# Two-pass sums of the stick and of the query/key squares, three mask matmuls in place of four, and the final norm's product on POOL, in a two-block decoder kernel

## The reference

```python
q = rms_norm(q.reshape(bsz, seq, ATTN_HEADS, HEAD_DIM), q_norm_g[layer])
k = rms_norm(k.reshape(bsz, seq, ATTN_HEADS, HEAD_DIM), k_norm_g[layer])
...
z = jnp.einsum("bqhd,bkhd->bhqk", qb, kb) * scale
mask = s_idx < t_idx
log_beta = jax.nn.log_sigmoid(z)
log_one_minus = jnp.where(mask, jax.nn.log_sigmoid(-z), 0.0)
tail = lax.cumsum(log_one_minus, axis=3, reverse=True) - log_one_minus
weights = jnp.where(mask, jnp.exp(log_beta + tail), 0.0)
outs.append(jnp.einsum("bhqk,bkhd->bqhd", weights, vb))
```

## Time and profile before

| | us |
|---|---|
| median of three runs | 1236.39 |
| the profiled execution | 1236.73 |
| its span, first to last instruction | 1235.0 |
| outside the span | 1.73 |
| PE busy | 1223.8 (99%) |
| DVE, ACT, POOL busy | 601.2, 505.1, 574.2 |

### The profile page before, as it was taken

How to read it: one execution, slowest core, us unless ns; L and a number is a source line. 1 busy time by engine, 2 the same in 40 slices (tenths; PEclk the granted TensorE clock), 3 DMA queues, 4 the chain that set the end, 5 groups by cost and what they waited for, 6 DMA issues and landing times.

```text
span 1235.0 us, 16489 instructions
## 1 busy us (share of the span) xinstructions
PE 1223.8 (99%) x5598; PEld 1004.6 (81%) x5598; DVE 601.2 (49%) x877; ACT 505.1 (41%) x674; POOL 574.2 (46%) x465
## 2 busy tenths in 40 slices
PE   9999999999999999999999999999999999999998
PEld 7888888888888888888888886768888888888887
DVE  6782435434653166414575879785334213321431
ACT  7532543343443144313473237666333223332331
POOL 5775553233445344453465441134454444444444
PEclk9999999999999999999999999999999999999999
DMA  8343332112333322232133321102232323223222
GB/s 298 124 145 126 118 103 69 51 69 68 102 102 104 102 85 93 94 119 84 64 124 104 101 86 51 35 18 85 71 104 98 117 88 102 86 85 120 81 76 81
DMA packets 34034, 118.41 MB, mean 96 GB/s; under 512 B 4032, under 2 KB 4160, under 8 KB 33856
## 3 DMA queue, kind: packets, MB, share of 16 engines
q1 hardware_dynamic: 33696, 117.49, 28.6%
q10 hardware_dynamic: 288, 0.24, 0.1%
HBM read 115.61 MB, written 2.10 MB: 95 GB/s over the span
## 4 chain that ended last, share of the span: by engine, by line
PE 95%; ACT 2%; DVE 1%; POOL 1%; issue 1%; DMA 0%; SPq 0%; POOLq 0%; ACTq 0%; DVEq 0%
PE ps L1240 29%; PE ps L1241 29%; PE ps L1242 29%; PE ps L1562 1%; PE ps L1407 1%; PE ps L1545 1%; PE ps L1298 1%; PE ps L1297 1%; PE ps L1296 1%; PE ps L1518 0%; PE ps L1306 0%; POOL w_lo L363 0%; PE ps L1603 0%; ACT slab L654 0%; POOL squares L431 0%
## 5 line engine op out<-in xcount | busy, mean ns | idle before, releaser
L363 POOL TENSOR_TENSOR w_lo<-w_raw,w_hi 128x512 fp32r<-128x512 f32 x430 | 555.3, 1315 | 621.8 <-ACT w_hi L464 355.7
L1240 PE MATMUL ps<-xg_hi,w_hi 128*128 128x512 f32 x960 | 375.7, 391 | 0.0
L1242 PE MATMUL ps<-xg_hi,w_lo 128*128 128x512 f32 x960 | 373.7, 389 | 0.0
L1241 PE MATMUL ps<-xg_lo,w_hi 128*128 128x512 f32 x960 | 373.6, 389 | 0.0
L1240 PE MATMUL ps<-y_hi,w_hi 128*128 128x512 f32 (+1 forms) x608 | 230.8, 380 | 0.0
L1241 PE MATMUL ps<-y_lo,w_hi 128*128 128x512 f32 (+1 forms) x608 | 229.8, 378 | 0.0
L1242 PE MATMUL ps<-y_hi,w_lo 128*128 128x512 f32 (+1 forms) x608 | 229.8, 378 | 0.0
L1240 PEld LDWEIGHTS ps<-xg_hi,w_hi 128*128 128x128 f32 x960 | 180.3, 188 | 37.8 <-issue 0.8
L1242 PEld LDWEIGHTS ps<-xg_hi,w_lo 128*128 128x128 f32 x960 | 180.2, 188 | 37.5
L1241 PEld LDWEIGHTS ps<-xg_lo,w_hi 128*128 128x128 f32 x960 | 180.3, 188 | 37.3 <-issue 0.5
L464 ACT ACTIVATE w_hi<-w_raw 128x1024 fp32r<-128x1024 f32 x124 | 130.5, 1053 | 126.0 <-PE ps L1242 126.0
(11 more groups left out here) (210 smaller groups left out, 1058.1 us busy)
## 6 DMA issues: line engine op xcount, KB each, us to landing
w_raw<-weights SPq DMA_DIRECT2D x199, 512.0 KB, 3.3
w_raw<-weights SPq DMA_DIRECT2D x16, 384.0 KB, 2.9
out_t<-h SPq DMA_DIRECT2D x8, 256.0 KB, 2.1
h<-x_t SPq DMA_DIRECT2D x3, 512.0 KB, 8.4
slab<-mem_t SPq DMA_DIRECT2D x2, 512.0 KB, 10.1
slab<-mats_in SPq DMA_DIRECT2D x1, 1024.0 KB, 7.3
w_raw<-weights SPq DMA_DIRECT2D x2, 256.0 KB, 3.9
h<-x_t SPq DMA_DIRECT2D x2, 256.0 KB, 4.4
```

Source lines behind the costliest of these rows:

```text
L363: nc.gpsimd.tensor_tensor(w_lo[:, s, half], w_raw[:, s, half], w_hi[:, s, half].bitcast(F32), ALU.subtract).then_inc(done, 1)
L1240: pe.matmul(out, w[0], x[0], start=first, stop=False)
L1241: pe.matmul(out, w[0], x[1], start=False, stop=False)
L1242: return pe.matmul(out, w[1], x[0], start=False, stop=last)
```

## The change

- The stick's running sums run in two fp32r passes. DVE copies the stick, rounded, into a free part of `y_hi` or `y_lo` (`stick_hi`), and then subtracts that from the stick in its own place (`stick_lo`). TensorE sums the high half over all later tiles, then the low half. The three adds on DVE and `later_sums` are gone, and TensorE covers 2560 columns a pass.
- The sums of the query and key squares take the same form. ACT makes the square twice, once rounded to fp32r and once in fp32, and POOL makes the residue.
- The masks of a head take three matmuls in place of four; the middle one writes two tiles of 128 columns at once.
- The final norm's product on `h` moves from DVE (after the last head) to POOL, two tiles behind each of the last four query/key blocks. Its gain moves into the residual add before the second feed-forward part.
- Three 128x128 constants are rounded once, early in the kernel.

```diff
+            weights_lo_for(GLU, QK - GLU)
+            pool.wait_ge(spread_copied, NORM_FINAL + 1)
+            for t in range(8):
+                pool.wait_ge(qk_square_r, t + 1)
+                pool.wait_ge(qk_square, t + 1)
+                nc.gpsimd.tensor_tensor(sq_lo[:, t % 2, :], sq[:, t % 2, :], qk_square_hi(t).bitcast(F32),
+                                        ALU.subtract).then_inc(qk_square_lo, 1)
+                weights_lo_next(QK + t)
+                for m in (2 * (t - 4), 2 * (t - 4) + 1) if t >= 4 else ():
+                    nc.gpsimd.tensor_tensor(h[:, m, :], h[:, m, :], final_bc[:], ALU.mult).then_inc(final_done, 1)
...
-                nc.scalar.activation(sq[:, t % 2, :], (q2, k2)[t % 2][:, t // 2, :], ACT.Square).then_inc(qk_square, 1)
+                values = (q2, k2)[t % 2][:, t // 2, :]
+                nc.scalar.activation(qk_square_hi(t), values, ACT.Square).then_inc(qk_square_r, 1)
+                nc.scalar.activation(sq[:, t % 2, :], values, ACT.Square).then_inc(qk_square, 1)
...
+                    if norm == NORM_TWO:
+                        nc.vector.scalar_tensor_tensor(out=new, in0=h[:, m, :], scalar=col("final_norm_g", m), in1=new,
+                                                       op0=ALU.mult, op1=ALU.add).then_inc(summed, 1)
...
                 for n, c in enumerate(log_parts(hd), log_parts_ahead(hd)):
                     dve.wait_ge(s_log, n + 1)
...
                     nc.vector.tensor_tensor(t[:, c], z_of(hd)[:, c], t[:, c], ALU.max).then_inc(s_stick, 1)
-                    dve.wait_ge(s_stick, hd + 1)
+                    dve.wait_ge(s_stick, n + 1)
                     if hd >= 2:
                         dve.wait_ge(s_cum, 2 * (hd - 1))
...
+                    nc.vector.tensor_copy(hi[:, c], t[:, c]).then_inc(s_hi, 1)
+                    dve.wait_ge(s_hi, n + 1)
+                    nc.vector.tensor_tensor(lo[:, c], t[:, c], hi[:, c].bitcast(F32), ALU.subtract).then_inc(s_lo, 1)
...
             pair_values_lo(2)
             s_softplus(7)
             ln_centre()
-            final_norm(range(DT))
...
-                pe.wait_ge(qk_square, t + 1)
-                pe.matmul(ps[:, QK_BANK[t], :], pair_ones[:], sq[:, t % 2, :], start=True, stop=True).then_inc(qk_sums, 1)
+                pe.wait_ge(qk_square_r, t + 1)
+                pe.matmul(ps[:, QK_BANK[t], :], pair_ones_r[:], qk_square_hi(t), start=True, stop=False)
+                pe.wait_ge(qk_square_lo, t + 1)
+                pe.matmul(ps[:, QK_BANK[t], :], pair_ones_r[:], sq_lo[:, t % 2, :], start=False, stop=True).then_inc(qk_sums, 1)
...
+                def sums_into(tile, stick):
+                    bank, at, n = TILES[tile]
+                    bank += 3 * (hd % 2)
+                    mm = pe.matmul(ps[:, bank, at:at + n], neg_tri_r[:], stick[:, AT[tile]:AT[tile] + n], start=False, stop=True,
+                                   skip_group_check=True)
+                    for later in range(tile + 1, ST):
+                        n = TILES[later][2]
+                        mm = pe.matmul(ps[:, bank, at + (later - tile) * P:at + (later - tile) * P + n], neg_ones_r[:],
+                                       stick[:, AT[later]:AT[later] + n], start=False, stop=True, skip_group_check=True)
+                    return mm
...
+                if hd != SPLIT_HEAD:
+                    ready(s_hi, 0)
+                    for group in tiles:
+                        for tile in group:
+                            sums_into(tile, stick_hi(hd))
+                    ready(s_lo, 0)
+                    for group in tiles:
+                        for tile in group:
+                            mm = sums_into(tile, stick_lo(hd))
+                        mm.then_inc(s_cum, 1)
```

More of the change, by code:

```diff
@@ L165, in build @@
         y_lo = sb("y_lo", [P, DT, SEQ], F32R)
-        slab = sb("slab", [P, 28 * SEQ])
+        with nc.sbuf_tensor("slab", [P, 28 * SEQ], F32) as slab:
+            pass
+        slab_r = sb("slab_r", [P, 28 * SEQ], F32R)
         memg_hi = y_hi[:, 4:8, :].rearrange("p a (b t) -> p (a b) t", b=2)
@@ L205, in build @@
         STICK = SEQ * ST - P * (ST * (ST - 1) // 2)
-        stick_slab = slab[:, 20 * SEQ:20 * SEQ + 3 * STICK].rearrange("p (b t) -> p b t", t=STICK)
+        stick_slab, stick_slab_lo = (t[:, 20 * SEQ:20 * SEQ + 3 * STICK].rearrange("p (b t) -> p b t", t=STICK)
+                                     for t in (slab, slab_r))
         cols = sb("cols", [P, N_COLS])
@@ L224, in build @@
         neg_ones = sb("neg_ones", [P, P])
-        squares = sb("squares", [P, 5 * SEQ])
+        with nc.sbuf_tensor("squares", [P, 5 * SEQ], F32) as squares:
+            pass
+        squares_r = sb("squares_r", [P, 5 * SEQ], F32R)
         stick_last = squares[:, 2 * SEQ:2 * SEQ + STICK]
-        sq = squares[:, 0:2 * SEQ].rearrange("p (a t) -> p a t", t=SEQ)
+        stick_last_lo = squares_r[:, 2 * SEQ:2 * SEQ + STICK]
+        sq, sq_lo = (t[:, 0:2 * SEQ].rearrange("p (a t) -> p a t", t=SEQ) for t in (squares, squares_r))
         ssq = squares[:, 2 * SEQ:4 * SEQ].rearrange("p (a t) -> p a t", t=SEQ)
-        later_sums = sb("later_sums", [P, 2, 3 * P])
+        pair_ones_r = sb("pair_ones_r", [P, P], F32R)
+        neg_tri_r = sb("neg_tri_r", [P, P], F32R)
+        neg_ones_r = sb("neg_ones_r", [P, P], F32R)
         rstd_bc = sb("rstd_bc", [P, SEQ])
@@ L820, in residual @@
                     dve.wait_ge(blocks_done, first + m + 1)
-                    nc.vector.tensor_tensor(new, new, h[:, m, :], ALU.add).then_inc(summed, 1)
+                    if norm == NORM_TWO:
+                        nc.vector.scalar_tensor_tensor(out=new, in0=h[:, m, :], scalar=col("final_norm_g", m), in1=new,
+                                                       op0=ALU.mult, op1=ALU.add).then_inc(summed, 1)
+                    else:
+                        nc.vector.tensor_tensor(new, new, h[:, m, :], ALU.add).then_inc(summed, 1)
                     if m > 0:
@@ L1547, in pair_scores @@
                 for hd in heads:
[L1548 to L1552, removed]
-            def s_cumulate(hd):
[L1556 to L1587, removed]
-                else:
-                    first_tile()
-                    other_tiles()
@@ new lines, in pair_scores @@
+                    bank = 3 * (hd % 2)
+                    pe.matmul(ps[:, bank, 0:P], ident_r[:], far_below_r[:], start=False, stop=False, skip_group_check=True)
+                    pe.matmul(ps[:, bank + 1, :].rearrange("p (a t) -> p a t", t=P)[:, 0:4:3, :], ident_r[:],
+                              far_below_r[:].rearrange("p (a t) -> p a t", a=1).broadcast_to([P, 2, P]), start=False, stop=False,
+                              skip_group_check=True)
+                    pe.matmul(ps[:, bank + 2, 0:P], ident_r[:], far_below_r[:], start=False, stop=False,
+                              skip_group_check=True).then_inc(s_z, 1)
@@ L1621, in _ @@
             qk_block(1)
+            pe.wait_ge(rounded, 5)
             qk_sum(0)
```

49 lines of the change are left out of this document (28 added, 21 removed).

## The result

| | us | |
|---|---|---|
| before, median of 4 runs beside it | 1236.82 | 1236.01 to 1237.41 |
| after, median of 4 runs | 1251.05 | 1250.84 to 1251.52 |
| ratio | 1.0116 | 95% interval 1.0099 to 1.0134 |
| span of the profiled execution | 1249.1 | 1235.0 before |

What follows compares the result with a forecast made beforehand. It took the kernel as bound by TensorE, with DVE nearly as full in the attention stage. DVE's +13.7 up to head 6's maximum and +1.0 in the tail gave +14.7 on 1236.39, so 1251 us, range 1239 to 1259.

Steps and rivals of the forecast that it cites:

- DVE sets the stage's end: Attention stage: from head 0 on TensorE waits for DVE, so the sum goes along DVE.
- DVE's own new work, 8.6 us for six heads: Before head 6's maximum: copy 0.82 plus subtraction 1.48 less adds 0.87, so 1.43 us more a head.
- 12 of 16 POOL instructions at 1.0 us: Attention stage: 12 of POOL's 16 new instructions meet a ready DVE instruction and cost it 1.0 us each.
- Free time left, 12.1 us: DVE up to head 6's maximum: of 19.0 us free, 12.1 stay once waits for TensorE's blocks vanish.
- the 6.9 for blocks: DVE's waits for TensorE's blocks before head 6's maximum, 6.9 us, vanish because DVE is now the later one.
- Head 6's maximum 13.7 later, the tail 1.0, in sum 14.7: DVE needs 105.3 us against 91.6 up to head 6's maximum, +13.7; heads 6 and 7 add +1.0.
- Head 0's stick 3.8 us later: Head 0: taps start some 1.5 us later and wait 2 to 3 us for three POOL instructions.
- TensorE's idle time 28 us: TensorE from 722 us to the stage's end: idle 4.0 + 9.5 + 14.7 = 28 us.
- The rival of the clock: TensorE's clock falls during longer waits before sums of heads 0, 1 and 6: adds 3 to 6, 1254 to 1260; chance 0.15.
- Half of it beside DVE's lag: One or two TensorE blocks at 1.2 GHz take 5.5 us more each; half beside DVE's lag, so 3 to 6 added.
- Half of it: Attention stage: only 3 to 5 of 16 POOL instructions are met; 13.7 falls to about 5.7, 1238 to 1245; chance 0.17.
- the gain stays: DVE's 11.5 us fits its free 19.0, POOL's falls into gaps: 1233, or up to 1236; chance 0.12 faster, 0.04 no change.

Runs made afterwards that it cites:

- the maximum made twice: Stick's maximum repeated for heads 0 to 5, 8.9 us more DVE work: 1238.84 us on the kernel before, 1256.94 us on the changed kernel.
- the stick on four heads: Kernel before with three masks, final norm's product on POOL eight blocks earlier, and two-pass stick on heads 2 to 5 only: 1234.67 us, ratio 0.9985.
- masks and early product alone: Kernel before with three masks for four and the final norm's product on POOL, eight blocks earlier than in the changed kernel: 1235.90 us, ratio 0.9992.
- the stick and the early product: Changed kernel with square sums as before, no residue, and the final norm's product on POOL eight blocks earlier: 1239.18 us, ratio 1.0025.

## Why the prediction was right

The path was right, and so were the sizes in the large: 14.7 us were forecast and 14.2 measured. That they lie so close is partly luck, for errors in the parts cancelled.

- *DVE sets the stage's end.* Right. The chain lies on DVE from 750 to 828 with one detour over ACT, and the same 8.9 us of DVE work cost 5.9 here and 2.2 before.
- *DVE's own new work, 8.6 us for six heads.* 9.2. The cast and the subtraction were right, 0.83 and 1.49 against 0.82 and 1.48; the old adds were too dear at 0.87 a head, since a pair of them takes 0.49 to 0.50 and all three 0.78.
- *12 of 16 POOL instructions at 1.0 us.* Right in its sum (12.1), not in its places. It assumed that the casts would be met as the subtractions are, and they are (1.85 against 0.83). The Trainium skill (SBUF — State Buffer, Who interferes with whom) says that copies and casts can enter a mode with two ports and then can contend with GpSimd; this trace agrees for the cast. By the same section a DVE instruction with both inputs in SBUF contends with a GpSimd one that reads SBUF, and one with at most one SBUF input, outside those modes, doesn't: the 33 PSUM taps of 21.99 us agree.
- *Free time left, 12.1 us.* 11.6 by the table, 11.3 of it in five waits, one of them 3.33 for the norm at 792.41. Right in the sum, again not in the parts: of the 6.9 for blocks, which were to vanish, 4.0 stayed (two blocks before any stick). The 3.1 for ACT's logarithms, which were to stay, vanished, and those for its norms fell from 8.6 to 7.3. That these cancel is luck.
- *Head 6's maximum 13.7 later, the tail 1.0, in sum 14.7.* 13.2, 0.9 and 14.1 by the spans; 14.2 by the medians.
- *Head 0's stick 3.8 us later.* Wrong in its path. The taps started 1.6 later, as said, but lost nothing to POOL: POOL waited. The maximum came 1.6 later, and the cast behind it was held up by 0.8 instead. TensorE waited 1.41 for it where 3.5 was forecast, and 1.06 for head 1's where it was 2.5. For head 6 it was 4.65 against 5 to 6. The last two forecasts, 2.5 and 5 to 6, stand in the prediction without a working.
- *TensorE's idle time 28 us.* It was 17.1. The gain itself was sized well: two heads' sums took 5.47 us, 2.73 a head against 2.82. What is missing went into the clock, which was short by 11.9 us. Of these, 2.2 fell into the 4.4 us at half the clock in which TensorE was idle anyway, so about 9.7 us went into longer matmuls, and 17.1 + 9.7 = 26.8. The loss of time of TensorE is near the forecast one; over a third of it stands in the profile as busy.
- *The rival of the clock.* Its condition came true, three times, and its price did not: the falls lay within DVE's lag, and a kernel without those three, its clock short by 6.6 us less in all, was 0.05 us faster, which is no difference. "Half of it beside DVE's lag" was where it went wrong; as far as these runs can tell, all of it was.
- *Half of it* and *the gain stays*: neither came. A gain stayed only in another kernel, with the stick on the middle heads, where the added DVE work (6.9 us) is about what its waits hold. For *the gain stays* the prediction took TensorE to wait already for the sticks of heads 0, 1, 6 and 7; it waited for those of 0, 1 and 7.

Not tried: an order in which POOL's residues stand behind the maxima alone. What decides which of DVE and POOL goes first when both stand ready stays open: the 1.27 us of POOL became 2.92 at one place, and at others DVE lost 1.0 instead.

## What to carry to other kernels

A kernel at 99% TensorE can still be set by another engine in one stage, so before moving work off TensorE, add up the other engine's waits in just that stage. Here DVE had 19 us free by the table. What its busy time grew by, less the time by which head 6's maximum came later, is what could be used of that: 4.7 us with the maximum made twice, 6.3 with the stick on four heads (against masks and early product alone), 8.4 with the stick and the early product, 7.4 in the changed kernel. So less than half. What was put in up to that (the stick on four heads) stands in a kernel that gained 2.0 us, 0.7 of which it had without it; what went beyond cost its length. To find such a number directly, give the engine a known amount of useless work and see what share comes through: 2.2 of 8.9 us before, 5.9 of 8.9 after. And put work for POOL beside DVE instructions that have an input in PSUM: eight products cost 4.6 us beside SBUF taps and nothing measurable beside PSUM ones.

## What the runs showed of the hardware

- DVE's row of taps, one right behind the other, kept a ready POOL instruction out until the first DVE instruction with a PSUM input (2.92 us for 1.27). In the kernel without residues a `w_lo` pair took 2.90 us there, for 2.50. Beside `w_lo` pairs DVE lost 0.8 to 1.1 us each, and at 760.27 the pair lost 1.85 too (4.35 us for 2.50).
- A granted clock of 0.50 beside waits of 1 to 5 us makes lost time look busy. The stretch from 754 to 766 has 9.97 busy us for 41 matmuls at 0.57 in the changed kernel, and 9.11 for 53 at 1.00 in the one with repeated matmuls. The Trainium skill (TensorE: Matmul & The Clock Gate, What's actually happening) says that activity is what releases the throttle; the kernel that kept TensorE active agrees in these stretches.
- A matmul of 128 columns was started both 0.11 and 0.06 us ahead of the next (785.97, 786.03 and 786.14 in the changed kernel), so a pass took 1.32 to 1.39 us, where the forecast had 1.41.
